# Eighty DMA issues of a decoder step's retention heads: from SyncE's queue to GpSimd's

## The chip, the cores and the metric

The kernel runs on one core of a Trainium2 chip. The metric is the device time of one execution in microseconds (us). The engines carry the profile's names: PE is TensorE (PEld its weight loads), DVE is VectorE, ACT is ScalarE, POOL is GpSimd and SP is SyncE, which computes nothing and issues DMAs.

## The reference

One inference step through two layers of a decoder: 528 prompt rows (16 learned meta tokens and 512 tokens) and 8 sample rows of one new token each, 1024 wide, in float32. Layer 0 mixes tokens by retention with four heads, layer 1 by a short convolution; each is followed by a gated MLP with a width-3 causal convolution. The part that matters here is retention, in which each head h holds a state of 256 x 512 for each of the 8 samples:

```
scores = einsum(q, k) * decay_mask
inner  = einsum(scores, v)
cross  = einsum(q, s_prev) * cross_decay
kv     = einsum(k * k_decay, v)
s_new  = exp(log_gamma * L) * s_prev + kv
...
return (silu(g) * o) @ w_out, s
```

For a sample L is 1, so its new state is the decayed old one plus the outer product of its k and v. The states (8 samples x 4 heads x 512 KB) are read from and written to DRAM, and the prompt's own state (512 KB for each head) is written too.

## The kernel before

The weight matrices are cut into 228 units of 128 x 1024 elements (512 KB). SP loads a unit into one of two `w_raw` buffers; ACT rounds it to `w_hi`, DVE subtracts to `w_lo` (four buffers each), and PE multiplies with both parts (three products for each tile of weights). A `w_raw` buffer is free again when ACT and DVE have read it: `load` (L289 to L297) waits for `hi_ready` and `lo_ready`. In the heads units 6 to 9 wait for `tail_read` besides, a product that PE makes from `w_raw` itself.

A head takes 16 units: 0 to 3 for q and k, 4 to 7 for v, 8 to 11 for the gate, 12 to 15 for the output. SP's queue runs its program in order, and the head's order is written out by hand in `head` on SP (L327 to L357): the units 0 to 5, the decay table, the eight sample states (L338, each after the store of the same buffer in the head before), units 6 to 10, then the sample rows of v to a scratch in DRAM (L343, after `v_tail`), a wait for that store, two broadcasts of the scratch to all 128 partitions (`v_bcast`, L347), units 11 to 13, the prompt's state (L351, after `kv_ready`), the eight new sample states (L354, each after its `s_upd`), and units 14 and 15.

Who uses what these DMAs bring: ACT and DVE fold the old states with the decayed q (L917, L1307), and PE sums the folds (L509). ACT makes the outer products of k and the broadcast v (`outer`, L948, two instructions for each sample; the first four samples wait for the first half of `v_bcast`, the others for the second), and DVE adds them to the states (`update`, L1351). On ACT `outer(0)` stands before the rounding of unit 11 and `outer(2)` to `outer(5)` between the copies of PE's results (L982); on DVE the sum of the prompt's state (L1369, `kv_ready`) follows the `w_lo` of unit 11, and PE waits for `kv_ready` before its third group of inner products. ACT waits for `kv_sent`, the landing of the prompt's state, before it writes squares over the same buffer (L989). After the last head ACT waits for all state stores.

POOL sets constants at the start and, before the change, issues a single DMA, that of `y_sample` at the very end.

Of the kernel before, what the change touches and what calls it, by code (L numbers as in the profile page):

```python
# [36 lines left out]
P = 128  # L37
D = 1024
KD = D // P
N_META, SEQ, NB = 16, 512, 8  # L40
TP = N_META + SEQ
T = TP + NB
HEADS, DK, DV = 4, 256, 512
# [54 lines left out]
def build(nc, io):  # L98
# [8 lines left out]
    with ctx:  # L107
# [22 lines left out]
        KV = TMP[:].rearrange("p a n -> p (a n)")[:, 2 * T:2 * T + 2 * DV]  # L130
# [3 lines left out]
        VSCR = nc.dram_tensor("v_scratch", (NB, DV), F32, kind="Internal").ap()  # L134
# [4 lines left out]
        with ExitStack() as s2:  # L139
            with ExitStack() as s3:  # L140
                VB = sb("v_bcast", [P, NB, DV], scope=s3)
            ZRH = sb("ret_z_hi", [P, 4, N_RET], F32R, scope=s2)
            ZRL = sb("ret_z_lo", [P, 4, N_RET], F32R, scope=s2)
            S = sb("states", [P, NB, 2 * DV], scope=s2)
            O = sb("q_k_or_out", [P, 4, T], scope=s2)
            Q, K = O[:, 0:2, :], O[:, 2:4, :]
            V = sb("v_rows", [P, 5, DV], scope=s2)
# [20 lines left out]
        with ExitStack() as s5:  # L168
# [8 lines left out]
        s_in = [sem(f"s_in{b}") for b in range(NB)]  # L177
        s_out = [sem(f"s_out{b}") for b in range(NB)]
        v_sent, kv_sent, copied, sent = (
            sem("v_sent"), sem("kv_sent"), sem("copied"), sem("sent"))  # L180
        vb_in = [sem(f"vb_in{half}") for half in range(2)]
# [72 lines left out]
        @block.gpsimd  # L254
        def _(pool):

            pool.memset(IDENT[:], 0.0).then_inc(const_ready, 1)  # L257
            pool.memset(MEAN_D[:], 1.0 / D).then_inc(const_ready, 1)  # L258
            pool.memset(MEAN_V[:], 1.0 / DV).then_inc(const_ready, 1)  # L259
            pool.memset(EPST[:], EPS).then_inc(const_ready, 1)  # L260
            pool.memset(HH[:, KD * T:].bitcast(F32), 0.0).then_inc(const_ready, 1)  # L261
            pool.memset(HL[:, KD * T:].bitcast(F32), 0.0).then_inc(const_ready, 1)  # L262
            pool.memset(HT[:], 0.0).then_inc(const_ready, 1)  # L263
            pool.memset(TMP[:, 3, 0:NB], 0.0).then_inc(const_ready, 1)
            pool.wait_ge(const_ready, 1)
            pool.affine_select(out=IDENT[:], in_=IDENT[:], compare_op=ALU.not_equal, fill=1.0, base=0,  # L266
                               pattern=[[-1, P]], channel_multiplier=1).then_inc(const_ready, 1)
            pool.memset(SEEDT[:, 0:1], 0.0).then_inc(unit_done, NS)  # L268
            pool.memset(SEEDT[:, 1:2], 0.0).then_inc(hi_ready, NR)  # L269
            pool.memset(SEEDT[:, 2:3], 0.0).then_inc(lo_ready, NR)  # L270
            pool.memset(SEEDT[:, 3:4], 0.0).then_inc(up_read, SEED)  # L271
            pool.memset(SEEDT[:, 4:5], 0.0).then_inc(sc_read, SEED)

            pool.memset(ONE_OF[:], 0.0).then_inc(const_ready, 1)  # L274
            pool.memset(KT[:].bitcast(F32), 0.0).then_inc(const_ready, 1)  # L275
            pool.memset(QL[:, :, N_LATE:], 0.0).then_inc(const_ready, 1)  # L276
            pool.wait_ge(const_ready, N_CONST + 1)
            for g in range(2):
                pool.memset(ONE_OF[:, g, 24 + 4 * g:26 + 4 * g], 1.0).then_inc(const_ready, 1)  # L279


            pool.wait_ge(ys_out, 1)
            pool.dma_start(io["y_sample"], YS[:].rearrange("p k b -> p (k b)")).then_inc(ys_sent, 16)


        @block.sync
        def _(sp):

            def load(c, m=0, i=0):  # L289

                need = m * i + (c + 1)
                sp.wait_ge(hi_ready, need)
                sp.wait_ge(lo_ready, need)
                if c == U_SC_IN + 4:
                    sp.sem_inc(head_stored, 1)
                src = w_all[bass.ds(m * i + c, 1)].rearrange("o p n -> (o p) n")
                sp.dma_start(RAW[:, c % NR, :], src).then_inc(raw_in[c % NR], 16)  # L297

            def in_heads(h, n):
                if 6 <= n <= 9:  # L300
                    sp.wait_ge(tail_read, 4 * h + (n - 5))
                load(n, U_HEAD, h)

            def x_tile(k):
                sp.dma_start(X[:, k, :], io["x_all"][:, k, :]).then_inc(x_in[k], 16)

            st_in = io["state_ret"][0].rearrange("b h (i e) v -> b h i (e v)", e=2)
            st_out = io["ret_s"][0].rearrange("b h (i e) v -> b h i (e v)", e=2)
            kv_dst = io["ret_p"][0, 0].rearrange("h (i e) v -> h i (e v)", e=2)

            for n in range(2):
                sp.dma_start(RAW[:, 0, 256 * n:256 * n + 256], w_all[0, :, 256 * n:256 * n + 256]).then_inc(part_in[n], 16)
                x_tile(n)
            sp.dma_start(RAW[:, 0, 512:], w_all[0, :, 512:]).then_inc(raw_in[0], 16)
            x_tile(2)
            x_tile(3)
            in_heads(0, 1)
            for k in range(4, KD):
                x_tile(k)
            in_heads(0, 2)  # L320
            sp.dma_start(COS[:], io["cos"]).then_inc(tab_in, 16)
            sp.dma_start(SIN[:], io["sin"]).then_inc(tab_in, 16)
            in_heads(0, 3)
            sp.dma_start(CD[:], io["model_consts"]).then_inc(const_in, 16)
            sp.dma_start(CF[:], io["ffn_consts"]).then_inc(ffn_in, 16)

            def head(h, first):  # L327
                for n in range(4 if first else 0, 6):
                    in_heads(h, n)
                if first:  # L330
                    sp.wait_ge(ss_sum, 7)
                else:
                    sp.wait_ge(s_upd, NB * h)
                sp.dma_start(DEC[:], io["decay"][h]).then_inc(dec_in, 16)
                for b in range(NB):
                    if not first:
                        sp.wait_ge(s_out[b], 16 * h)
                    sp.dma_start(S[:, b, :], st_in[b, h]).then_inc(s_in[b], 16)  # L338
                for n in range(6, 11):
                    in_heads(h, n)  # L340

                sp.wait_ge(v_tail, 4 * h + 4)
                sp.dma_start(VSCR, V[16:24, 4, :]).then_inc(v_sent, 16)  # L343
                sp.wait_ge(v_sent, 16 * h + 16)
                for half in range(2):
                    b = half * NB // 2
                    sp.dma_start(VB[:, b:b + NB // 2, :], VSCR[b:b + NB // 2, :].partition_broadcast(P)).then_inc(vb_in[half], 16)  # L347
                for n in range(11, 14):
                    in_heads(h, n)
                sp.wait_ge(kv_ready, h + 1)  # L350
                sp.dma_start(kv_dst[h], KV).then_inc(kv_sent, 16)  # L351
                for b in range(NB):
                    sp.wait_ge(s_upd, NB * h + (b + 1))
                    sp.dma_start(st_out[b, h], S[:, b, :]).then_inc(s_out[b], 16)  # L354
                for n in range(14, 16):
                    in_heads(h, n)

            for h in range(HEADS):
                head(h, h == 0)

            for l in range(2):
                sp.dma_start(io["ffn_s0"][l], io["state_ffn"][l, :, 1, :]).then_inc(copied, 16)
            sp.dma_start(io["conv_s0"], io["state_conv"][0, :, 1, :]).then_inc(copied, 16)

            def ffn_units(l):
                with sp.Fori(0, JF // 2) as i:
                    for n in range(4):
                        load(U_FFN_IN[l] + n, 4, i)
                for n in range(22):
                    load(U_FFN_OUT[l] + n)  # L370
                    if n == 4:
                        sp.wait_ge(gf_kept, JF * (l + 1))
                        sp.dma_start(io["ffn_last"][l], GF[l][:].rearrange("p t j -> p (t j)")).then_inc(sent, 16)

            ffn_units(0)
            with sp.Fori(0, 4) as i:
                for n in range(6):
                    load(U_SC_IN + n, 6, i)
            for n in range(8):
                load(U_SC_OUT + n)  # L380
            sp.wait_ge(gc_kept, KD)
            sp.dma_start(io["conv_last"], GC[:].rearrange("p t j -> p (t j)")).then_inc(sent, 16)
            ffn_units(1)

            for b in range(4):
                sp.wait_ge(rows_dve, FIN_ROWS[b])
                sp.wait_ge(rows_act, FIN_ROWS[b])
                sp.dma_start(io["y_prompt"][0, P * b:P * (b + 1), :], YN[:, b, :]).then_inc(sent, 16)
            sp.wait_ge(copied, 48)
            sp.wait_ge(sent, 16 * (4 + 2 + 1))  # L390
            sp.wait_ge(ys_sent, 16)
# [1366 lines left out]
```

## Time and profile before

| | us |
|---|---|
| median of 3 runs (lowest, highest) | 1457.04 (1456.8, 1457.08) |
| the profiled execution, its own time | 1458.02 |
| its span, first to last instruction | 1454.7 |
| PE busy in the span | 1449.2 |
| DVE, ACT, POOL busy | 799.9, 543.2, 2.9 |
| granted TensorE clock, mean | 1.000 |

The profiled execution took 3.32 us more than its span, and 0.98 us more than the median. A head is some 120 us long (the folds of three heads begin at 158.75, 278.63 and 398.87 us), and the four heads end before 500 us; the rest, two MLPs and the short convolution, has none of the DMAs that the diff moves.

### The profile page before, as it was taken

Reading aid. Unit: us, or ns where it says so; the run is one execution under the profiler, and the core shown is the slowest. Engines: PE = TensorE matmul, PEld = TensorE weight load, DVE = VectorE, ACT = ScalarE, POOL = GpSimd, SP = SyncE. Lnnn points to the kernel's source line nnn. Section 1 sums busy time; section 2 is a strip of 40 time slices with the busy share of each in tenths; the row PEclk is TensorE's granted clock in tenths of the full one; section 3 lists DMA queues with packets and bytes.
Section 4 is the critical chain, followed back from the end, with each engine's and each line's share of the span. In section 5 each row is a group of like instructions: output and inputs, shape, how many; then the busy total and the mean of one; then the engine's idle time right before and its main releaser. Section 6 shows DMA issues by size and latency. Waiting matters only on the chain.

```text
span 1454.7 us, 27349 instructions
## 1 busy us (share of the span) xinstructions
PE 1449.2 (100%) x11428; PEld 1395.2 (96%) x11428; DVE 799.9 (55%) x1066; ACT 543.2 (37%) x776; POOL 2.9 (0%) x24
## 2 busy tenths in 40 slices
PE   9999999999999999999999999999999999999998
PEld 9699789879979999999999999999999999999998
DVE  7885577468458855555542427444565555553222
ACT  5552273264155543333331314222343333332222
POOL 0000000000000000000000000000000000000000
PEclk9999999999999999999999999999999999999999
DMA  8445253463444322222222222232223222222221
GB/s 302 149 186 192 96 225 107 180 232 104 166 162 178 115 89 87 89 98 87 87 93 100 87 88 88 88 97 92 89 89 100 87 87 99 88 87 101 92 88 59
DMA packets 47742, 171.94 MB, mean 118 GB/s; under 512 B 5608, under 2 KB 6248, under 8 KB 46624
## 3 DMA queue, kind: packets, MB, share of 16 engines
q1 hardware_dynamic: 47488, 170.76, 33.8%
q8 instruction: 62, 1.02, 0.3%
q14 instruction: 16, 0.13, 0.0%
q0 software_dynamic: 32, 0.03, 0.0%
q10 hardware_dynamic: 144, 0.00, 0.0%
HBM read 149.44 MB, written 21.55 MB: 118 GB/s over the span
## 4 chain that ended last, share of the span: by engine, by line
issue 100%; POOL 0%; POOLq 0%
POOLq L107 0%; POOL ident L266 0%; POOL h_tail L263 0%; POOL k_tail_stack L275 0%; POOL mean_v L259 0%; POOL ident L257 0%; POOL h_hi L261 0%; POOL h_lo L262 0%; POOL sample_ones L274 0%; POOL sample_ones L279 0%; POOL mean_d L258 0%; POOL late_q_decayed L276 0%; POOL seed L268 0%; POOL seed L269 0%; POOL seed L271 0%
## 5 line engine op out<-in xcount | busy, mean ns | idle before, releaser
L846 ACT ACTIVATE w_hi<-w_raw 128x1024 fp32r<-128x1024 f32 x227 | 240.1, 1059 | 671.4 <-PE ps L405 469.1
L405 PE MATMUL ps<-h_hi,w_hi 128*128 128x264 f32 (+2 forms) x2300 | 468.3, 285 | 0.4 <-DVE h_lo L1184 0.4
L405 PE MATMUL ps<-h_lo,w_hi 128*128 128x264 f32 (+2 forms) x2300 | 465.4, 284 | 0.0
L405 PE MATMUL ps<-h_hi,w_lo 128*128 128x264 f32 (+2 forms) x2300 | 464.9, 283 | 0.0
L1159 DVE TENSOR_TENSOR w_lo<-w_raw,w_hi 128x1024 fp32r<-128x1024 f32 x227 | 277.0, 1222 | 334.5 <-ACT w_hi L846 334.2
L405 PEld LDWEIGHTS ps<-h_hi,w_hi 128*128 128x128 f32 x2300 | 355.8, 188 | 1.5 <-issue 0.8
L405 PEld LDWEIGHTS ps<-h_hi,w_lo 128*128 128x128 f32 x2300 | 355.5, 188 | 0.0
L405 PEld LDWEIGHTS ps<-h_lo,w_hi 128*128 128x128 f32 x2300 | 355.3, 188 | 0.0
L695 PE MATMUL ps<-z_hi,w_lo 128*128 128x264 f32 (+1 forms) x704 | 144.7, 283 | 0.0
L695 PE MATMUL ps<-z_lo,w_hi 128*128 128x264 f32 (+1 forms) x704 | 144.6, 283 | 0.0
L695 PE MATMUL ps<-z_hi,w_hi 128*128 128x264 f32 (+1 forms) x704 | 144.6, 283 | 0.0
L695 PEld LDWEIGHTS ps<-z_hi,w_lo 128*128 128x128 f32 x704 | 110.1, 189 | 0.0
L695 PEld LDWEIGHTS ps<-z_lo,w_hi 128*128 128x128 f32 x704 | 109.9, 188 | 0.0
L695 PEld LDWEIGHTS ps<-z_hi,w_hi 128*128 128x128 f32 x704 | 109.8, 188 | 0.0
L1482 DVE TENSOR_TENSOR tmp<-ps,rms 128x524 f32<-128x524 f32 (+1 forms) x44 | 28.8, 696 | 76.1 <-PE ps L405 76.1
L1463 DVE TENSOR_TENSOR tmp<-ps,rms 128x528 f32<-128x528 f32 (+1 forms) x44 | 29.0, 701 | 67.9 <-PE ps L405 67.8
L530 PE MATMUL ps<-w_hi,h_hi 128*128 128x512 f32 x128 | 52.2, 408 | 0.0
L405 PE MATMUL ps<-ret_z_hi,w_lo 128*128 128x264 f32 x256 | 52.0, 285 | 0.0
L405 PE MATMUL ps<-ret_z_hi,w_hi 128*128 128x264 f32 x256 | 51.9, 284 | 0.0
L405 PE MATMUL ps<-ret_z_lo,w_hi 128*128 128x264 f32 x256 | 51.8, 284 | 0.0
L530 PE MATMUL ps<-w_hi,h_lo 128*128 128x512 f32 x128 | 50.5, 395 | 0.0
L530 PE MATMUL ps<-w_lo,h_hi 128*128 128x512 f32 x128 | 50.5, 394 | 0.0
(205 smaller groups left out, 1407.7 us busy)
## 6 DMA issues: line engine op xcount, KB each, us to landing
w_raw<-in_w_units_dram SPq DMA_DIRECT2D x227, 512.0 KB, 3.3
states<-in_state_ret_dram SPq DMA_DIRECT2D x32, 512.0 KB, 8.5
out_ret_s_dram<-states SPq DMA_DIRECT2D x32, 512.0 KB, 4.6
v_bcast<-v_scratch SPq DMA_DIRECT2D x8, 1024.0 KB, 5.6
x_res<-in_x_all_dram SPq DMA_DIRECT2D x8, 268.0 KB, 6.0
out_ret_p_dram<-tmp SPq DMA_DIRECT2D x4, 512.0 KB, 3.7
out_y_prompt_dram<-y_rows SPq DMA_DIRECT2D x4, 512.0 KB, 2.6
decay<-in_decay_dram SPq DMA_DIRECT2D x4, 299.5 KB, 3.8
```

Of the source, the lines that this page charges most:

```text
L405: out = mm(PS[:, 2 * s + half, at:at + n_col], a, b[:, lo:lo + n_col], start=first and n == 0, stop=last and n == 2)
L530: out = mm(PS[:, 2 + b, :], a, c, start=k == 0 and q == 0, stop=k == KD - 1 and q == 2)
L695: out = mm(PS[:, 2 * DOWN[t] + half, to:to + n_col], a, z[:, j, lo:lo + n_col], start=j == 0 and q == 0, stop=j == JF - 1 and q == 2)
L846: fn(WH[:, c % NS, :], RAW[:, c % NR, :], ACT.Copy).then_inc(hi_ready, 1)
L1159: tt(WL[:, c % NS, :], RAW[:, c % NR, :], WH[:, c % NS, :].bitcast(F32), ALU.subtract).then_inc(lo_ready, 1)
L1463: tt(halves(TMP[:, t, 0:n_in]), slot(PAIR_A[t], w), halves(R[:, c0:]), ALU.mult).then_inc(up_read, 1)
L1482: tt(halves(TMP[:, t, 4:n_in]), slot(PAIR_B[t], n_out // 2), halves(R[:, c0 + 4:]), ALU.mult).then_inc(gate_read, 1)
```

## The change

The state loads, the scratch store, the wait for it, the two broadcasts, the prompt state's store and the sample states' stores leave SP's program and become a stream on POOL, head after head, with the same semaphores and in the same order among themselves. SP keeps the weight units and the decay table, so that its units 6 to 15 follow one another with no other wait than their own. POOL issues a head's state loads right behind the stores of the head before, where SP had units 14 and 15, the next head's units 0 to 5 and the decay table between them.

```diff
--- before.py
+++ after.py
@@ -279,6 +279,36 @@
                 pool.memset(ONE_OF[:, g, 24 + 4 * g:26 + 4 * g], 1.0).then_inc(const_ready, 1)
 
 
+            st_in = io["state_ret"][0].rearrange("b h (i e) v -> b h i (e v)", e=2)
+            st_out = io["ret_s"][0].rearrange("b h (i e) v -> b h i (e v)", e=2)
+            kv_dst = io["ret_p"][0, 0].rearrange("h (i e) v -> h i (e v)", e=2)
+
+            def state_stream(h):
+
+                def broadcast():
+                    for half in range(2):
+                        b = half * NB // 2
+                        pool.dma_start(VB[:, b:b + NB // 2, :], VSCR[b:b + NB // 2, :].partition_broadcast(P)).then_inc(vb_in[half], 16)
+
+                for b in range(NB):
+                    if h > 0:
+                        pool.wait_ge(s_out[b], 16 * h)
+                    elif b == 0:
+                        pool.wait_ge(ss_sum, 7)
+                    pool.dma_start(S[:, b, :], st_in[b, h]).then_inc(s_in[b], 16)
+                pool.wait_ge(v_tail, 4 * h + 4)
+                pool.dma_start(VSCR, V[16:24, 4, :]).then_inc(v_sent, 16)
+                pool.wait_ge(v_sent, 16 * h + 16)
+                broadcast()
+                pool.wait_ge(kv_ready, h + 1)
+                pool.dma_start(kv_dst[h], KV).then_inc(kv_sent, 16)
+                for b in range(NB):
+                    pool.wait_ge(s_upd, NB * h + (b + 1))
+                    pool.dma_start(st_out[b, h], S[:, b, :]).then_inc(s_out[b], 16)
+
+            for h in range(HEADS):
+                state_stream(h)
+
             pool.wait_ge(ys_out, 1)
             pool.dma_start(io["y_sample"], YS[:].rearrange("p k b -> p (k b)")).then_inc(ys_sent, 16)
 
@@ -303,10 +333,6 @@
 
             def x_tile(k):
                 sp.dma_start(X[:, k, :], io["x_all"][:, k, :]).then_inc(x_in[k], 16)
-
-            st_in = io["state_ret"][0].rearrange("b h (i e) v -> b h i (e v)", e=2)
-            st_out = io["ret_s"][0].rearrange("b h (i e) v -> b h i (e v)", e=2)
-            kv_dst = io["ret_p"][0, 0].rearrange("h (i e) v -> h i (e v)", e=2)
 
             for n in range(2):
                 sp.dma_start(RAW[:, 0, 256 * n:256 * n + 256], w_all[0, :, 256 * n:256 * n + 256]).then_inc(part_in[n], 16)
@@ -332,27 +358,7 @@
                 else:
                     sp.wait_ge(s_upd, NB * h)
                 sp.dma_start(DEC[:], io["decay"][h]).then_inc(dec_in, 16)
-                for b in range(NB):
-                    if not first:
-                        sp.wait_ge(s_out[b], 16 * h)
-                    sp.dma_start(S[:, b, :], st_in[b, h]).then_inc(s_in[b], 16)
-                for n in range(6, 11):
-                    in_heads(h, n)
-
-                sp.wait_ge(v_tail, 4 * h + 4)
-                sp.dma_start(VSCR, V[16:24, 4, :]).then_inc(v_sent, 16)
-                sp.wait_ge(v_sent, 16 * h + 16)
-                for half in range(2):
-                    b = half * NB // 2
-                    sp.dma_start(VB[:, b:b + NB // 2, :], VSCR[b:b + NB // 2, :].partition_broadcast(P)).then_inc(vb_in[half], 16)
-                for n in range(11, 14):
-                    in_heads(h, n)
-                sp.wait_ge(kv_ready, h + 1)
-                sp.dma_start(kv_dst[h], KV).then_inc(kv_sent, 16)
-                for b in range(NB):
-                    sp.wait_ge(s_upd, NB * h + (b + 1))
-                    sp.dma_start(st_out[b, h], S[:, b, :]).then_inc(s_out[b], 16)
-                for n in range(14, 16):
+                for n in range(6, 16):
                     in_heads(h, n)
 
             for h in range(HEADS):
```

## Rows read from the trace of the kernel before

**Rows 1.** Page, part 1: busy us (share of the span), instructions.

```profile
PE 1449.2 (100%) x11428; PEld 1395.2 (96%) x11428; DVE 799.9 (55%) x1066; ACT 543.2 (37%) x776; POOL 2.9 (0%) x24
```

**Rows 2.** Waits of PE's weight loads, 40 to 500 us: total, times, longest us.

```profile
PEld ps L573 <- issue: 12.5, 52, 0.2
...
PEld ps L501 <- DVE q_k_or_out L1277: 0.7, 2, 0.4
PEld ps L501 <- DVE q_k_or_out L1276: 0.4, 1, 0.4
PEld ps L501 <- DVE w_lo L1159: 0.3, 1, 0.3
```

**Rows 3.** Waits of SP's queue, whole span, same columns.

```profile
SPq L354 <- DVE states L1351: 65.3, 28, 9.9
```

**Rows 4.** Timeline of SP's queue, second head: start, length in us, count.

```profile
177.16 0.29 SPq L343 DMA_DIRECT2D v_scratch<-v_rows  x1
180.33 0.81 SPq L347 DMA_DIRECT2D v_bcast<-v_scratch  x2
189.03 6.15 SPq L297 DMA_DIRECT2D w_raw<-in_w_units_dram  x3
195.94 0.34 SPq L351 DMA_DIRECT2D out_ret_p_dram<-tmp  x1
```

**Rows 5.** Timeline of SP's queue, end of the second head.

```profile
217.44 36.09 SPq L297 DMA_DIRECT2D w_raw<-in_w_units_dram  x8
...
254.05 4.80 SPq L338 DMA_DIRECT2D states<-in_state_ret_dram  x8
```

**Rows 6.** Timeline of DVE, second head, same columns.

```profile
187.73 1.23 DVE L1159 TENSOR_TENSOR w_lo<-w_raw,w_hi 128x1024 fp32r<-128x1024 f32 x1
...
194.70 1.22 DVE L1369 TENSOR_TENSOR tmp<-ps,tmp 128x1024 f32<-128x1024 f32 x1
```

**Rows 7.** POOL's one DMA before: ns min/median/max, and its landing.

```profile
L283 POOL DMA_DIRECT2D out_y_sample_dram<-y_samples x1: 672/672/672, 1451.9 to 1451.9; - x1
...
DMA to landing us min/median/max: 2.3/2.3/2.3
```

**Rows 8.** The state stores on SP, same columns.

```profile
L354 SPq DMA_DIRECT2D out_ret_s_dram<-states x32: 332/422/1202, 76.0 to 456.7; - x32
```

**Rows 9.** Stretches of the second head; PEclk, DMA share, GB/s come last.

```profile
183.00:186.00 3.00, 3.00 (x19) 2.19 (x18) 1.93 (x7) 2.87 (x8) 0.00 (x0) 1.00 1.01 421
186.00:189.00 3.00, 3.00 (x9) 1.33 (x8) 2.86 (x5) 2.03 (x4) 0.00 (x0) 1.00 0.20 82
```

**Rows 10.** Timeline of ACT, second head; in brackets the idle time before.

```profile
190.13 1.32 ACT L948 ACTIVATE gate<-v_bcast,dec_k 128x512 f32<-128x512 f32 x2
192.47 1.06 ACT L846 ACTIVATE w_hi<-w_raw 128x1024 fp32r<-128x1024 f32 x1 [1.01 <-DMA w_raw<-in_w_units_dram]
...
209.89 1.70 ACT L989 ACTIVATE tmp<-q_k_or_out 128x528 f32<-128x528 f32 x3
```

**Rows 11.** Timeline of PE's weight loads, second head.

```profile
197.09 0.72 PEld L599 LDWEIGHTS ps<-scores,v_rows 128*128 128x128 f32 x4
```

**Rows 12.** Timeline of ACT, second head's end and third head's start.

```profile
231.79 2.00 ACT L846 ACTIVATE w_hi<-w_raw 128x1024 fp32r<-128x1024 f32 x2
...
278.63 2.56 ACT L917 ACTIVATE tmp<-states,dec_q 128x512 f32<-128x512 f32 x4 [15.20 <-DVE dec_q L1300]
```

**Rows 13.** Timeline of SP's queue, first head.

```profile
23.24 4.49 SPq L338 DMA_DIRECT2D states<-in_state_ret_dram  x8
```

**Rows 14.** Timeline of ACT, first head.

```profile
42.28 2.57 ACT L917 ACTIVATE tmp<-states,dec_q 128x512 f32<-128x512 f32 x4 [0.87 <-DVE dec_q L1300]
```

**Rows 15.** Timeline of DVE, last part of the second head.

```profile
213.75 2.47 DVE L1351 SCALAR_TENSOR_TENSOR states<-states,decay,gate 128x1024 f32<-128x1024 f32 x2
...
229.08 0.70 DVE L1389 TENSOR_TENSOR gate<-ps,rms 128x528 f32<-128x528 f32 x1
```

**Rows 16.** Timeline of PE's weight loads, the same part.

```profile
229.94 0.31 PEld L405 LDWEIGHTS ps<-ret_z_hi,w_hi 128*128 128x128 f32 x2
```

## Prediction

> **What bounds the kernel now.** I read the page's first part to see which engine fills the span, then who made PE wait inside the heads, then SP's queue and the timelines of one head around each moved DMA. The page shows PE busy for 1449.2 of a span of 1454.7 us [rows 1]. A busy PE can still hide waits, so the second view counts: between 40 and 500 us, where all the moved DMAs lie, PE's weight loads waited for another engine 0.7 + 0.4 + 0.3 = 1.4 us in all, and each of those waits was for DVE [rows 2]. The commonest row, "issue", is 0.2 us at a time between plain matmuls and names no releaser. So PE sets the time, and data from a DMA never came late to it. Whatever is done to the queues can give back about 1.4 us in the heads and no more.
>
> SP looks otherwise: it waited 65.3 us on the state stores alone [rows 3], with weight units queued behind. The reader should ask whether one of those units was due. Take the second head. The units behind the broadcast go out from 189.03 us [rows 4]; the DVE instruction that frees their buffer ran from 187.73 for 1.23 us, to 188.96 [rows 6]. Unit 14, behind the last state store, went out at 217.44 [rows 5]; the buffer was freed by the `w_lo` that follows the two state updates begun at 213.75 and lasting 2.47 us [rows 15], and a `w_lo` takes 1.23. So SP was back from its waits when each buffer came free, within 0.1 us. The waits on SP held up nothing.
>
> **The change, part by part.** *Removed from SP:* 20 issues a head, 80 in all, of some 0.42 us each [rows 8], and their waits. Worth 0 by the two comparisons above; the cover is that the buffers are freed by DVE no earlier.
>
> *Added on POOL:* the same 80 issues. The only price in the trace is its one DMA before, 0.672 us for the issue and 2.3 us to landing [rows 7]. 80 x 0.672 = 54 us of an engine that was busy 2.9 [rows 1]; in itself this costs nothing. What counts is lateness of each kind.
>
> *Scratch and broadcast* are the tight ones. Before, the scratch store went out at 177.16 (0.29 us), the first broadcast at 180.33 (0.81 for two), and the transfers ran at 421 GB/s until 186 and had almost ended by 187 (a share of 0.20 over the next 3 us) [rows 4, 9]. ACT reads the first half at 190.13 without having waited [rows 10]: some 3.5 us of cover for both halves. Behind it ACT rounds unit 11, which had 1.01 us to spare for its DMA [rows 10], and DVE's `kv_ready` comes at 194.70 + 1.22 = 195.92, 1.2 us before PE wants it at 197.09 [rows 6, 11]. PE would notice a broadcast that is 3.5 + 1.0 + 1.2 = 5.7 us late, and only the rest beyond that. Expected lateness: (0.672 - 0.29) + (0.672 - 0.41) = 0.6 us for two issues, from below perhaps less than nothing, since the store no longer stands behind a weight unit in SP's queue (it took 180.33 - 177.16 = 3.2 us there). From above, if a landing on POOL's queue cost its 2.3 us on top of SP's each time, 0.6 + 4.6 = 5.2. Both ends stay under 5.7. I take 0.6, the value of the row with the same kind of issue, and a loss of 0.
>
> *Prompt state:* issued at 195.94, wanted by ACT at 209.89 [rows 4, 10]. 14 us of cover against 0.3 us more of issue and up to 5 us of landing. 0.
>
> *State stores and next loads:* the loads move from 254.05 [rows 5] to right behind the last store, that is from about 217 on; 8 x 0.672 = 5.4 us of issues, and 4 MB at 421 GB/s [rows 9] take 10 us, done by about 230. ACT wants them at 278.63, when it had waited 15.2 us for DVE and not for them [rows 12]. They now run beside units 14 and 15, loaded from 217.44 and wanted by ACT at 231.79 [rows 5, 12]; 4 MB and 1 MB together need 12 us at that rate and end at 229 or 230. 0, with 2 us to spare. In the first head the loads went out at 23.24, in 4.49 us, and the first fold is at 42.28, after a wait for DVE [rows 13, 14]: 5.4 us of issue in place of 4.49 lies in 19 us of cover. 0.
>
> *Sum:* -1.4 us at best, 0 likeliest, on a span of 1454.7. With the 3.32 us around the span the profiled execution would stay at 1458.0; the median of the runs, 0.98 lower, is what is asked: 1457.0 us.
>
> The rows show DVE busy without a gap from the state updates at 213.75 to 229.78 [rows 15], just where POOL will now issue its loads. A rule speaks against that: the Trainium skill (SBUF — State Buffer, section "SBUF: two separate sides") says that descriptors of a GpSimd DMA are written by GpSimd's cores, which are locked out while VectorE runs a two-port operation, and gives 620 ns alone against about 3100 ns beside a copy. No row here shows a GpSimd DMA beside VectorE work. By that figure, as an estimate, store and broadcast would be 2 x 2.5 = 5.0 us later on top of the 0.6, which uses up all the cover, and the sum would be 0 with nothing to spare; rival B is what lies just beyond.
>
> **Rivals.** *A, VectorE is held while POOL issues (slower).* Each POOL issue stops DVE while it lasts. For it: DVE is the one engine whose work at that place is tight. Its gate product at 229.08 ends at 229.78 and PE loads the weights that need it at 229.94 [rows 15, 16], 0.16 us to spare. The last two state stores and eight loads fall in the unbroken stretch. If each holds DVE for x, a head loses 10x - 0.16, three heads have loads behind them, and the last has the two stores only: 3 (10x - 0.16) + 2x - 0.16 = 32x - 0.64. At x = 0.672, the whole issue, that is +20.9 us, 1478. It decides (2.9 us) from x = 0.11 us on. Against it: the trace shows POOL and DVE side by side nowhere, so neither end is excluded; but an issue works on no tile of DVE's, and I take x near 0. The same section of the Trainium skill (SBUF — State Buffer) has the lock work both ways, for a VectorE instruction with two SBUF inputs only against a GpSimd operation that reads SBUF; by that x would be 0 for most of this stretch, which no run here shows.
>
> *B, the broadcast comes too late (slower).* If each of the two steps on POOL cost 4 us more than on SP, the lateness would be 8.0, 2.3 past the cover, in four heads: +9.2 us, 1466. It decides from 5.7 + 0.7 = 6.4 us of lateness. Against it: the one POOL landing in the trace took 2.3 us.
>
> *C, SP's freedom pays (faster).* If the 65.3 us of waits had held up units that PE needed, PE would show waits; it shows 1.4 us. All of that gives 1455.6, still no difference that can be told. More than 2.9 us faster would need waits that the profile counts as busy.
>
> *D, the queue's release is real but nothing on PE's path uses it:* that is the forecast itself.
>
> **How the numbers follow.** About 0.2%, 2.9 us, is what a measurement of this kernel can tell from no change. The forecast, PE unchanged, gets 0.80; it covers -1.4 to +2.9 us. A gets 0.10 and B 0.05, together 0.15 for slower; C, through something that the rows hide, 0.05 for faster. The time is that of the forecast, 1457.0. The range begins at 1455.5, the forecast less all of PE's waits, and reaches past the forecast's end (1459.9) into the weaker half of A and B, to 1463 (x = 0.2 in A gives +5.8).
>
> **What would show it right or wrong.** Right: PE's waits on other engines between 40 and 500 us stay at 1 to 2 us, the weight units of the heads go out within 0.1 us of the `w_lo` that frees them as before, the loads of the second head's successor start near 217 us, and `outer(0)` starts without idle time. A would show as longer DVE instructions or gaps between 213 and 230 us, with PE waiting for DVE. B would show as ACT's L948 waiting for `v_bcast`, then PE for L1369. The first thing to make me wrong is a POOL issue that takes several times 0.672 us: the row that I lean on is one DMA of 32 KB, and the moved ones carry up to 1 MB.

## The result: 4.4 us slower, all of it behind the last instruction of the computation

The changed kernel took 1461.36 us (median of 8 runs, 1461.12 to 1462.09) against 1457.0 us of the kernel before beside it (8 runs, 1456.71 to 1457.43): a ratio of 1.003, 95% interval 1.0021 to 1.0039. The forecast was 1457.0, no change. The time lies inside the range of 1455.5 to 1463, but for a cause that no part of that range stood for. The profiled execution took 1461.18 us with a span of 1459.4, 4.7 more than the span before.

First the page, part 1, and the waits of PE's weight loads between 40 and 500 us (total, times, longest us), to set against [rows 1, 2]:

```profile
PE 1449.2 (99%) x11428; PEld 1395.2 (96%) x11428; DVE 800.1 (55%) x1066; ACT 543.0 (37%) x776; POOL 45.0 (3%) x104
```

```profile
PEld ps L579 <- issue: 12.5, 52, 0.2
...
PEld ps L507 <- DVE q_k_or_out L1283: 0.7, 2, 0.4
PEld ps L507 <- DVE q_k_or_out L1282: 0.4, 1, 0.4
PEld ps L507 <- DVE w_lo L1165: 0.3, 1, 0.3
```

PE is busy 1449.2 us as before, and its weight loads wait for another engine the same 0.7 + 0.4 + 0.3 us; its matmuls waited once for DVE besides, 0.2 us. Lines have moved by 6: L507 is the L501 of before. PE lost next to nothing where the DMAs were moved. So the reader goes to the other end, the last 8 us. The next two views are the block's closing instructions (line, engine, operation, then ns min/median/max, first and last start), of the kernel before and of the changed one:

```profile
L107 POOLq DRAIN  x1: 2437/2437/2437, 1451.9 to 1451.9; - x1
...
L107 SPq DRAIN  x1: 7/7/7, 1454.5 to 1454.5; - x1
L107 SPq EVENT_SEMAPHORE  x1: 17/17/17, 1454.6 to 1454.6; - x1
```

```profile
L107 POOLq DRAIN  x1: 7254/7254/7254, 1451.9 to 1451.9; - x1
...
L107 SPq DRAIN  x1: 7/7/7, 1455.1 to 1455.1; - x1
L107 SPq EVENT_SEMAPHORE  x1: 17/17/17, 1459.3 to 1459.3; - x1
```

POOL's queue closes with a DRAIN that begins with its last DMA issue, that of y_sample, at 1451.9 us in both kernels. Before, it lasted 2.44 us; now it lasts 7.25, which is 4.82 more. SP has seen all its landings by 1455.1, and the semaphores on which all engines meet are passed at 1459.3, against 1454.6. The waits of SP's queue and the last stretches (us, then busy time of PE, PEld, DVE, ACT, POOL; PEclk, DMA share, GB/s) show that all stand still:

```profile
SPq L107 <- PEq L107: 4.3, 1, 4.3
SPq L397 <- DMA out_y_sample_dram<-y_samples: 3.4, 1, 3.4
```

```profile
1452.00:1455.00 3.00, 0.00 (x0) 0.00 (x0) 0.00 (x0) 0.00 (x0) 0.47 (x1) 0.91 0.58 235
1455.00:1457.00 2.00, 0.00 (x0) 0.00 (x0) 0.00 (x0) 0.00 (x0) 0.00 (x0) 0.50 0.00 0
1457.00:1459.40 2.40, 0.00 (x0) 0.00 (x0) 0.00 (x0) 0.00 (x0) 0.00 (x0) 0.50 0.00 0
```

From 1455 on no engine computes and no DMA moves a byte (0 GB/s), so nothing is being waited for that carries data. The SP row names "PEq L107", one of the others at the same meeting; PE's own closing instruction began at 1448.8 and took 2.07 us in both kernels. The only instruction open in that stretch is POOL's DRAIN. Nor does every engine that issues DMAs end like this: SP, which issued over 250 in each kernel, has a closing DRAIN of 7 ns in both.

The heads, for the steps of the prediction. The timeline of POOL in the second head (start, length in us, count; idle time before in brackets) and the two groups of state DMAs on POOL (ns min/median/max, first and last start), beside [rows 4, 5, 8]:

```profile
177.47 0.51 POOL L300 DMA_DIRECT2D v_scratch<-v_rows  x1 [76.39 <-DVE v_rows L1332]
180.66 1.07 POOL L291 DMA_DIRECT2D v_bcast<-v_scratch  x2 [2.69 <-DMA v_scratch<-v_rows]
196.13 0.54 POOL L304 DMA_DIRECT2D out_ret_p_dram<-tmp  x1 [14.40 <-DVE tmp L1375]
...
217.09 4.27 POOL L298 DMA_DIRECT2D states<-in_state_ret_dram  x8
```

```profile
L298 POOL DMA_DIRECT2D states<-in_state_ret_dram x32: 527/530/680, 22.9 to 341.8; - x32
...
L307 POOL DMA_DIRECT2D out_ret_s_dram<-states x32: 531/531/536, 76.7 to 457.1; - x32
```

Timelines of ACT and of DVE in the same head, beside [rows 10, 15]:

```profile
190.18 1.32 ACT L954 ACTIVATE gate<-v_bcast,dec_k 128x512 f32<-128x512 f32 x2
192.39 1.06 ACT L852 ACTIVATE w_hi<-w_raw 128x1024 fp32r<-128x1024 f32 x1 [0.89 <-DMA w_raw<-in_w_units_dram]
```

```profile
213.80 2.48 DVE L1357 SCALAR_TENSOR_TENSOR states<-states,decay,gate 128x1024 f32<-128x1024 f32 x2
...
229.14 0.70 DVE L1395 TENSOR_TENSOR gate<-ps,rms 128x528 f32<-128x528 f32 x1
```

An issue on POOL takes 0.53 us, ACT reads the broadcast without idle time, and DVE's instructions are as long as before and at most 0.06 us later, with ten POOL issues among them.

### The profile page after: what moved, and what is told of

Its sections match the earlier page's. It is cut to its first block, busy times and chain, and to the rows that moved or that the text cites. A ratio compares the mean times of both kernels' runs of the same rounds, so it can differ in the third digit from the quotient of the medians.

```text
span 1459.4 us, 27349 instructions
## 1 busy us (share of the span) xinstructions
PE 1449.2 (99%) x11428; PEld 1395.2 (96%) x11428; DVE 800.1 (55%) x1066; ACT 543.0 (37%) x776; POOL 45.0 (3%) x104
## 3 DMA queue, kind: packets, MB, share of 16 engines
q0 software_dynamic: 11104, 44.14, 7.8%
q8 instruction: 63, 1.03, 0.3%
## 4 chain that ended last, share of the span: by engine, by line
issue 68%; PE 29%; DMA 1%; DVE 1%; ACT 0%; SPq 0%; POOLq 0%; POOL 0%; ACTq 0%; DVEq 0%
PE ps L411 16%; PE ps L536 6%; PE ps L579 2%; PE ps L608 1%; PE ps L569 1%; PE ps L605 1%; PE ps L610 1%; DMA w_raw<-in_w_units_dram 1%; PE ps L515 1%; PE ps L507 1%; PE ps L444 0%; PE ps L552 0%; DVE tmp L1313 0%; DVE states L1357 0%; ACT w_hi L852 0%
## 6 DMA issues: line engine op xcount, KB each, us to landing
states<-in_state_ret_dram POOLq DMA_DIRECT2D x32, 512.0 KB, 11.1
```

## The experiments

The theory after the result: POOL settles at its closing DRAIN every DMA that it issued, at a price for each, however long ago their data landed. The computation is over by then, so the price shows in full. Rivals: the DRAIN waits for y_sample alone, whose landing became slow (2.9 us against 2.3); or something else at the end is longer and the DRAIN only covers it; or the price goes by bytes or descriptors. N is the number of DMAs that POOL has issued since its last DRAIN, or since the start: 1 before, 81 after (80 moved, and y_sample). "Settle" is only a name here: what POOL does in this time no trace shows.

**The last store issued by SP, in the changed kernel.** POOL then has nothing to wait for behind its stream and can close early.

```diff
-            pool.wait_ge(ys_out, 1)
-            pool.dma_start(io["y_sample"], YS[:].rearrange("p k b -> p (k b)")).then_inc(ys_sent, 16)
...
+            sp.wait_ge(ys_out, 1)
+            sp.dma_start(io["y_sample"], YS[:].rearrange("p k b -> p (k b)")).then_inc(ys_sent, 16)
```

> The changed kernel with y_sample's store on SP, so that POOL's last DMA is a state store near 457 us. Theory (POOL's closing drain is long, because it settles the DMAs that POOL issued): the drain begins near 458 us and lies beside a thousand microseconds of PE's work; SP's end decides, at about 1454.5 to 1455 of span, and the median is 1456.8 to 1457.5. Rival (the 4.4 us were lost in the heads or by sharing the DMA engines): the median stays near 1461.4.

Measured: 1456.77 us against 1457.28, ratio 0.9998 (0.9989 to 1.0007). The loss is gone, and the DRAIN is still there, 1000 us earlier, beside PE's work (this kernel's closing instructions):

```profile
L107 POOLq DRAIN  x1: 7162/7162/7162, 456.9 to 456.9; - x1
```

Its 7.16 us for N = 80 has no y_sample in it, which rules out the late landing as the cause.

**The same exchange in the kernel before.** POOL issues no DMA at all (N = 0).

> The kernel before with y_sample's store on SP, so that POOL issues no DMA at all. Theory: POOL's closing drain is short and early, the end hangs on SP's last landing, and the median is 1456.5 to 1457.2. If POOL's way of issuing costs the end something by itself (rival: a fixed price of a POOL DMA at the end), it falls by 0.5 us or more below 1457.0.

Measured: 1457.1 against the same 1457.28, ratio 0.9998 (0.9989 to 1.0007). POOL's DRAIN took 0.387 us:

```profile
L107 POOLq DRAIN  x1: 387/387/387, 2.5 to 2.5; - x1
```

So moving y_sample is worth nothing by itself, and what the run above won back is the DRAIN's.

**A second drain in the middle.** y_sample stays on POOL; a drain is added behind the last head's stores.

```diff
             for h in range(HEADS):
                 state_stream(h)
 
+            pool.drain()
             pool.wait_ge(ys_out, 1)
```

> The changed kernel with one more drain on POOL, between the last state store and the wait for y_sample. Theory (a drain settles what was issued since the last one): the added drain takes about 5 us plus the landing of the last store, in the shade of PE; the closing one is back at 2.4 to 3 us in place of 7.25, and the median is 1456.8 to 1457.7. Rival (the closing drain is long for whatever the program has issued, or for y_sample's landing): 7.25 us again and 1461.4.

Measured: 1456.92 against 1457.28, ratio 0.9998 (0.9989 to 1.0007). The added drain and the closing one in its trace:

```profile
L312 POOLq DRAIN  x1: 7166/7166/7166, 456.9 to 456.9; - x1
```

```profile
L107 POOLq DRAIN  x1: 2445/2445/2445, 1451.7 to 1451.7; - x1
```

This separates the theory from the rivals. What was paid once is not paid again: the closing DRAIN is back at 2.44 us, with all 81 DMAs issued in the same places.

**No closing drain on POOL.** The changed kernel with `nc.Block(no_gpsimd_drain=True)`.

> The changed kernel without POOL's closing drain (the engines meet by semaphores alone; SP still waits for every store of the outputs that it waited for). Theory: the span ends some 0.2 to 0.4 us after SP's wait for y_sample, near 1455.2, and the median is 1457.0 to 1457.8. Rival (the drain only shows a delay that lies in the DMAs themselves): SP or another engine ends as late as before and the median stays near 1461.4.

Measured: 1457.39 against 1457.28, ratio 1.0003 (0.9994 to 1.0012), with no DRAIN of POOL in the trace and a span of 1454.9. Nothing else at the end had become longer.

**Tiny copies on POOL, in the kernel before.** Copies of 32 bytes within DRAM, into a scratch that nothing reads, issued in the first head behind `kv_ready`: first 80, then 160.

```diff
+            pool.wait_ge(kv_ready, 1)
+            for n in range(80):
+                pool.dma_start(TINY[n:n + 1, :], io["mix_gain"][0:1].rearrange("p k o -> p (k o)")).then_inc(tiny_in, 16)
+            pool.wait_ge(tiny_in, 16 * 80)
```

> The kernel before with 80 copies of 32 bytes from DRAM to a DRAM scratch that nobody reads, issued by POOL after the first kv_ready (near 76 us). Theory by count (a price for each DMA that POOL issued, (7.254 - 2.437) / 80 = 0.060 us): the closing drain is 7.2 us and the median 1461.4. Rival by volume (a price for each packet or byte; these are 80 packets and 2.6 KB against 11,104 and 44 MB): the drain stays at 2.4 to 2.5 us and the median at 1457.0.

> The same with 160 copies. Theory by count: a drain of 2.44 + 160 x 0.060 = 12.1 us and 1466.2. Rival by volume: 2.4 to 2.5 and 1457.0. Rival by a fixed price (whoever has issued more than a few DMAs pays once): the same as with 80.

Measured: with 80, 1464.41 against 1457.24, ratio 1.0053 (1.0036 to 1.007), and in the trace

```profile
L107 POOLq DRAIN  x1: 7291/7291/7291, 1454.1 to 1454.1; - x1
```

81 DMAs that moved 0.04 MB in 2592 packets (32 for each, not the one that was expected) took 7.29 us to settle; 81 that moved 44 MB in 11104 packets took 7.25 (part 3 of the pages). So neither bytes nor packets nor the state buffers matter. The median rose by 7.17 us, more than expected, because the copies also ran among the weight loads: from 96 to 106 us the DMA engines were full (a share of 1.00) at 118 GB/s, where before they had a share of 0.54 at 194, and PE was busy 2.9 us less in the first 130 us. The DRAIN began 2.2 us later than before, and 2.2 + (7.29 - 2.44) = 7.05.

With 160 the expectation missed: 1466.84, ratio 1.0072 (1.0055 to 1.0089), and a closing DRAIN of only 3.45 us where 12.1 was expected. POOL's timeline suggests why:

```profile
L107 POOLq DRAIN  x1: 3451/3451/3451, 1458.2 to 1458.2; - x1
```

```profile
75.56 65.60 POOL L286 DMA_DIRECT2D tiny<-in_mix_gain_dram  x128 [72.78 <-DVE tmp L1375]
150.75 16.36 POOL L286 DMA_DIRECT2D tiny<-in_mix_gain_dram  x32 [9.59 <-issue]
```

POOL issued 128, stood for 9.59 us, and issued the other 32. If it settled what it had in that pause, 32 + 1 were left at the end. The pause as settling is inferred from the count, not tried by itself. This run lost more in the heads: y_sample went out 6.3 us later than before, and its four runs lie between 1465.48 and 1469.94.

**State loads cut in two by partitions.** The changed kernel, each load as two of 64 partitions: N = 113, the same bytes. ACT, whose waits the fence leaves out, waits for both halves.

```diff
-                    pool.dma_start(S[:, b, :], st_in[b, h]).then_inc(s_in[b], 16)
+                    for p0 in (0, 64):
+                        pool.dma_start(S[p0:p0 + 64, b, :], st_in[b, h, p0:p0 + 64]).then_inc(s_in[b], 16)
...
```

> The changed kernel with each state load cut into two of 64 partitions: 32 issues more, the same bytes and rows. Theory by count: a drain of 7.25 + 32 x 0.060 = 9.2 us and 1463.3. Rivals by volume and by a fixed price: 7.25 us and 1461.4.

Measured: 1486.85 against 1457.24, ratio 1.0196 (1.0179 to 1.0213), 23.5 us above what was expected. The closing DRAIN:

```profile
L107 POOLq DRAIN  x1: 9867/9867/9867, 1476.9 to 1476.9; - x1
```

Its 9.87 us, where 9.2 was expected, are about what the count says, but it began 25 us late. The heads had lost that: the last state store went out at 482.1 us, against 457.1 in the changed kernel. The next three runs separate the two effects.

**Cut in two by columns, loaded in pairs, 20 tiny copies.** The first has N = 113 again but full 128 partitions; the second takes the count down, N = 65 with the same bytes; the third, 20 of the tiny copies above in the kernel before, has N = 21. The fence has the new issue of the first, then that of the second; the waits that go with them are left out.

```diff
+                    for c0 in (0, 512):
+                        pool.dma_start(S[:, b, c0:c0 + 512], st_in[b, h, :, c0:c0 + 512]).then_inc(s_in[b], 16)
...
+                    pool.dma_start(S[:, b:b + 2, :], st_in[b:b + 2, h].rearrange("b p x -> p b x")).then_inc(s_in[b], 16)
```

> The changed kernel with each state load cut in two by columns (all 128 partitions, 512 elements each) and not by partitions: 113 DMAs, as in the run with the loads cut by partitions. Count theory: closing drain 0.8 + 113 x 0.080 = 9.8 us, 2.6 above the changed kernel, median about 1464.0 if the 22 us lost in the heads of that run came from transfers of 64 partitions. Rival: they came from the number of DMAs on GpSimd, or from a load issued in two; then the heads lose about 22 us here too, and the median is about 1486.

> The changed kernel with each head's eight state loads issued as four, of two states each: the same bytes, 16 DMAs fewer, so 65 in place of 81 wait on GpSimd for the end. Count theory, with the price that 33, 81 and 113 DMAs gave (0.8 us and 0.080 us for each): closing drain 0.8 + 65 x 0.080 = 6.0 us in place of 7.25, median about 1460.1, 1.2 below the changed kernel. Rival, the drain goes by bytes or by the descriptors that these make: bytes and rows are the same, the drain stays at 7.25 us and the median at 1461.4.

> The kernel before with 20 copies of 32 bytes on GpSimd in the first head. Count theory: 0.8 + 21 x 0.080 = 2.5 us, no longer than the last store's own landing of 2.3 us needs, so the closing drain stays near 2.44 us and the median within 0.3 us of the kernel before, 1457.0 to 1457.5. Rival, every DMA adds to the 2.44 us that one DMA took: 2.44 + 20 x 0.080 = 4.0 us, median about 1458.7.

Measured, against 1456.88 of the kernel before: by columns 1464.41, ratio 1.0054 (1.004 to 1.0067); in pairs 1459.9, ratio 1.002 (1.0011 to 1.0029); 20 copies 1457.51, ratio 1.0004 (0.9994 to 1.0013). Their closing DRAINs, in this order, one fence for each kernel:

```profile
L107 POOLq DRAIN  x1: 9867/9867/9867, 1451.9 to 1451.9; - x1
```

```profile
L107 POOLq DRAIN  x1: 5951/5951/5951, 1451.9 to 1451.9; - x1
```

```profile
L107 POOLq DRAIN  x1: 2967/2967/2967, 1452.3 to 1452.3; - x1
```

All DRAINs by their count, one profiled execution each; the 33 is the count inferred above:

| N | 0 | 1 | 21 | 33 | 65 | 80 | 81 | 113 |
|---|---|---|---|---|---|---|---|---|
| us | 0.39 | 2.44 | 2.97 | 3.45 | 5.95 | 7.16, 7.17 | 7.25, 7.29 | 9.87 (both) |

From 65 to 113 the price is (9.87 - 5.95) / 48 = 0.082 us for each DMA, and that line, 0.65 + 0.0816 N, gives 7.18 for 80, 7.26 for 81 and 3.34 for 33. Below that it doesn't hold: it would give 2.36 for 21 and 0.73 for 1. At N = 1 the DRAIN ends near y_sample's landing, 2.3 us after its issue [rows 7]; at 21 it took 2.97, more than the line and more than that run's landing of 2.0, and my expectation there was 0.5 too low. What sets it between 1 and 33 stays open; the time of that run can't be told from no change. Taking 16 DMAs away with the same bytes cut the DRAIN by 1.30 and the loss from 4.4 to 3.0 us, as the count says.

The cut by columns also settles the 25 us: with as many DMAs as the cut by partitions it began its DRAIN at 1451.9, as in the changed kernel. Stretches right behind the second head's state loads, cut by partitions and then cut by columns:

```profile
230.00:235.00 5.00, 5.00 (x43) 5.00 (x42) 5.00 (x4) 2.79 (x4) 5.00 (x11) 1.00 0.94 253
```

```profile
225.00:230.00 5.00, 5.00 (x44) 5.00 (x43) 4.90 (x9) 1.80 (x4) 0.53 (x2) 1.00 1.03 419
```

The DMA engines are full in both (a share of 0.94 and 1.03), but halves of 64 partitions move 253 GB/s and whole transfers 419. The Trainium skill (SBUF — State Buffer, section "Door 1: The DMA port swizzle") says that partitions 0 to 63 reach only half of SBUF's DMA ports, so that a transfer of them gets little more than half the bandwidth; these two rows agree, at 0.60, though the ports themselves stand in no row. The loads then stayed longer in the way of the weight units: ACT's waits for `w_raw` between 40 and 500 us rose to 70.4 us from 42.5 in the changed kernel, and were 40.5 with the cut by columns. PE then stood for lack of input. At the first such place ACT waited for a unit, DVE's `w_lo` and the sum behind it (`x_res`, L1442) came late, and PE waited for that; the rows of ACT and of PE:

```profile
130.50 1.06 ACT L853 ACTIVATE w_hi<-w_raw 128x1024 fp32r<-128x1024 f32 x1 [10.60 <-DMA w_raw<-in_w_units_dram]
```

```profile
134.19 0.78 PE L412 MATMUL ps<-ret_z_hi,w_hi 128*128 128x264 f32 x2 [3.28 <-DVE x_res L1442]
```

The 130 us from this place on, about one head, in the kernel cut by partitions and then in the changed one:

```profile
130.00:260.00 130.00, 124.00 (x868) 110.35 (x866) 77.39 (x102) 53.68 (x77) 14.56 (x28) 0.97 0.51 158
```

```profile
130.00:260.00 130.00, 130.00 (x942) 116.75 (x941) 79.32 (x103) 53.91 (x77) 10.53 (x20) 1.00 0.43 159
```

That is 6.0 us of idle PE, and a mean granted clock of 0.97 in place of 1.00. The clock fell right behind the pause; the first 10 us of the stretch, cut by partitions:

```profile
130.00:135.00 5.00, 1.72 (x12) 1.54 (x11) 2.45 (x3) 1.58 (x2) 0.00 (x0) 0.82 0.75 210
135.00:140.00 5.00, 5.00 (x24) 5.00 (x24) 3.59 (x4) 1.59 (x2) 0.00 (x0) 0.50 0.45 146
```

At 0.50, the lower of the clock's two levels (1.2 GHz), a PE busy for all 5 us counts 24 matmuls; in the 5 us behind them, at 1.00 (2.4 GHz), it counts 43. From 0 to 390 us PE was busy 15.5 us less than in the changed kernel; the rest of the 25 us goes with the lower clock that followed the pauses (0.99, 0.97 and 0.96 in the three thirds, as an estimate 130 x 0.08 = 10 us).

## Why the prediction was wrong

**The step that failed** is "Added on POOL": "80 x 0.672 = 54 us of an engine that was busy 2.9 [rows 1]; in itself this costs nothing". It priced each DMA where it is issued, looked for lateness inside the heads, and took the end as given ("With the 3.32 us around the span the profiled execution would stay at 1458.0"). Each DMA also lengthens POOL's closing DRAIN, and that term, 0 in the sum, measured +4.82 us (the span rose by 4.7, the median by 4.36). Put in, the sum is 1457.0 + 4.8 = 1461.8, against 1461.36. The DRAIN was in the trace of before, 2.44 us long and the last thing to end beside y_sample's landing. With N = 1 its length could not give the price per DMA; but work that POOL does last, behind PE, had no cover to be hidden by, and its bound should have been asked for.

**Removed from SP: right.** SP issued the 16 weight units of a head waiting only on `w_lo` and PE, and PE's weight loads waited no longer. The 65.3 us [rows 3] had held up nothing. Rival C fell.

**Scratch and broadcast: right.** The first broadcast went out 0.33 us later than before (180.66 against 180.33), and the issue of both ended 0.59 later (181.73 against 181.14), where 0.6 was taken, of 5.7 us of cover. From store to broadcast it took 3.19 us on POOL and 3.17 on SP, so neither the gain nor the loss at the landing came that the prediction had as its two ends. `outer(0)` started at 190.18 against 190.13 without idle time [rows 10], and unit 11 behind it kept 0.89 of its 1.01 us. Rival B fell.

**Rival A fell too.** The loads went out at 217.09 us, 8 in 4.27, beside a VectorE that had no gap; its state updates took 2.48 us for two against 2.47, and the gate product began 0.06 us later [rows 15]. Nor did VectorE hold POOL: the 64 state DMAs took 0.53 us at the median and 0.68 at most. The lock-out that the Trainium skill describes (SBUF — State Buffer, section "SBUF: two separate sides") was not met here by any of them; beside the ten issues of this stretch VectorE ran two-input operations and a reciprocal, and no copy, the case for which the Trainium skill gives its 3100 ns.

**Prompt state, stores and loads: right.** The prompt state left at 196.13, 0.2 us later. The loads began where the forecast put them, and the third head's fold still waited 15.21 us for DVE, as in [rows 12].

So every term inside the heads held in what PE shows, the three rivals that were priced did not occur, and the one slower mechanism that did was not on the list. The weight of 0.80 for no change was too high for a list that looked only at the heads.

No version beat the kernel before. With y_sample on SP, or a drain behind the last head, the changed order ties with it (0.9998, 0.9989 to 1.0007, in both): the freed SP queue is worth nothing to PE, as the forecast had it, once the debt at the end is paid out of sight.

## What to carry to other kernels

Price a moved DMA three times: at its issue, at its landing, and at the close of the engine that issued it; the last was exposed here because POOL's final action is also the kernel's. For GpSimd it was 0.082 us a DMA between 65 and 113; it went out of the time when the engine's last DMA came early, and when it drained in mid-kernel under other work. When PE is as busy as before and the span is longer, read the closing instructions of every queue before looking for a stall inside.

## What the hardware did that was not expected

- From 65 DMAs on, the closing DRAIN of POOL goes by their number and not by their bytes, packets or age: 7.25 us for 81 DMAs of 44 MB, 7.29 for 81 of 0.04 MB, 80 of them done over 900 us earlier.
- POOL stopped by itself for 9.59 us after 128 DMAs in a row, in the one run that issued so many, and had 128 fewer to settle at the end, by the length of its DRAIN. The pause is near the line's 0.65 + 128 x 0.0816 = 11.1 us, but not on it, and stays unexplained.
- With copies of 32 bytes issued every 0.5 us, the share of the DMA engines was 1.00 in place of 0.54, and their rate 118 in place of 194 GB/s (96 to 106 us).
- Two transfers of 64 partitions in place of one of 128 lowered the rate in the same stretch of the head from 419 to 253 GB/s and made the heads 25 us longer. Two transfers of half the columns cost nothing there.
- The landing of y_sample issued by SP took 4.4 us in the profile of one of the two kernels that issue it there, and 2.6 in that of the other; what made the difference is not known.
